# A two-block transformer kernel on one core: a new setup around TensorE, and three waits of the layers put in another order

## The reference, cut to what matters

```python
for l in range(2):
    h = rmsnorm(x, norm_g[l]);  p = split(h @ w_in[l])
    o_a = mla(p.cq, p.ckv, p.krope, ...)            # q = rms(cq) @ w_uq ; k, v = rms(ckv) @ w_ukv
    o_b = diff_attn(p.b_q, p.b_k, p.b_v, ...)
    o_c = dsa(p.c_q, p.c_k, p.c_v, qidx, kidx, widx, topk=128)
    o_d = conv(p.d_b, p.d_c, p.d_h)
    x = x + concat(o_a*silu(gate_a), o_b*silu(gate_b), o_c*silu(gate_c), o_d*silu(gate_d)) @ w_out[l]
x = second_block(x, ...)
```

## Time and profile before

| what | value |
|---|---|
| median of 3 runs | 1811.5 us (1811.14 to 1812.63) |
| the profiled execution's own time | 1812.77 us |
| its span | 1810.9 us |
| PE busy / DVE / ACT / POOL | 99% / 58% / 41% / 22% |
| granted PE clock over the span | 0.997 |
| DMA | 165.53 MB, 91 GB/s over the span |

### The profile page before, as it was taken

How to read it: one execution, slowest core, us unless ns; L and a number is a source line. 1 busy time by engine, 2 the same in 40 slices (tenths; PEclk the granted TensorE clock), 3 DMA queues, 4 the chain that set the end, 5 groups by cost and what they waited for, 6 DMA issues and landing times.

```text
span 1810.9 us, 25324 instructions
## 1 busy us (share of the span) xinstructions
PE 1790.2 (99%) x9372; PEld 1447.0 (80%) x9372; DVE 1051.0 (58%) x2117; ACT 746.6 (41%) x1379; POOL 395.0 (22%) x235
## 2 busy tenths in 40 slices
PE   8999999999999999999999999999999999999998
PEld 5767778776777888888888878878888888888887
DVE  3879767587867764554433435555665655545333
ACT  5454554446455432322222355546444323323222
POOL 2345452444545220000000232130200200000000
PEclk9999999999999999999999999999999999999999
DMA  6222112322211242333333422223221333323332
GB/s 221 71 82 71 59 59 83 95 71 82 76 51 59 86 143 93 98 99 93 97 108 107 154 64 73 91 71 111 87 82 37 103 93 95 102 93 95 103 105 92
DMA packets 49621, 165.53 MB, mean 91 GB/s; under 512 B 5624, under 2 KB 6136, under 8 KB 49528
## 3 DMA queue, kind: packets, MB, share of 16 engines
q1 hardware_dynamic: 48232, 161.88, 28.7%
q10 hardware_dynamic: 1296, 2.42, 0.4%
HBM read 162.12 MB, written 2.17 MB: 91 GB/s over the span
## 4 chain that ended last, share of the span: by engine, by line
PE 93%; DVE 4%; issue 2%; ACT 1%; DMA 0%; POOL 0%; SPq 0%; DVEq 0%; ACTq 0%
PE proj L963 75%; PE o L1237 2%; PE turned L1213 2%; PE score L1187 1%; PE turned L1439 1%; PE score L1430 1%; PE proj L1360 1%; PE o L1465 1%; PE proj L1367 1%; PE score L1196 1%; PE turned L935 1%; PE o L1544 1%; DVE arena L2206 1%; PE turned L947 1%; PE score L1533 1%
## 5 line engine op out<-in xcount | busy, mean ns | idle before, releaser
L963 PE MATMUL proj<-hhi,whi 128*128 128x512 f32 x1464 | 584.9, 400 | 0.6 <-DVE tanh L2123 0.3
L963 PE MATMUL proj<-hhi,wlo 128*128 128x512 f32 x1464 | 571.7, 390 | 0.0
L963 PE MATMUL proj<-hlo,whi 128*128 128x512 f32 x1464 | 570.9, 390 | 0.0
L1632 ACT ACTIVATE whi<-ring 128x1024 fp32r<-128x1024 f32 x280 | 296.2, 1058 | 638.6 <-PE proj L963 632.9
L2068 DVE TENSOR_TENSOR wlo<-ring,whi 128x1024 fp32r<-128x1024 f32 x200 | 244.3, 1221 | 168.2 <-ACT whi L1632 167.6
L963 PEld LDWEIGHTS proj<-hhi,whi 128*128 128x128 f32 x1464 | 275.8, 188 | 59.5 <-issue 6.6
L963 PEld LDWEIGHTS proj<-hhi,wlo 128*128 128x128 f32 x1464 | 275.2, 188 | 58.8
L963 PEld LDWEIGHTS proj<-hlo,whi 128*128 128x128 f32 x1464 | 275.8, 188 | 52.9
L732 POOL TENSOR_TENSOR wlo<-ring,whi 128x1024 fp32r<-128x1024 f32 x80 | 193.5, 2420 | 406.3 <-ACT whi L1632 405.7
L744 POOL TENSOR_TENSOR prob<-prob 128x512 f32<-128x512 f32 x36 | 56.9, 1579 | 877.2 <-ACT prob L1628 877.2
L1658 ACT ACTIVATE prob<-prob,negmax 128x256 f32<-128x256 f32 (+3 forms) x208 | 114.3, 552 | 60.8 <-DVE negmax L2112 59.7
(11 more groups left out here) (304 smaller groups left out, 2394.3 us busy)
## 6 DMA issues: line engine op xcount, KB each, us to landing
ring<-wstream SPq DMA_DIRECT2D x288, 512.0 KB, 3.5
arena<-lines SPq DMA_DIRECT2D x28, 256.0 KB, 5.7
arena<-x ACTq DMA_DIRECT2D x4, 512.0 KB, 6.3
out<-arena SPq DMA_DIRECT2D x8, 256.0 KB, 2.7
arena<-mem SPq DMA_DIRECT2D x1, 1024.0 KB, 9.0
par<-params ACTq DMA_DIRECT2D x3, 74.0 KB, 1.8
arena<-hot SPq DMA_DIRECT2D x2, 80.0 KB
arena<-rope SPq DMA_DIRECT2D x1, 128.0 KB, 7.1
```

The source lines that it names most:

```text
L963: mm = pe.matmul(b, rounded(w), rounded(rhs(v, k)), start=(first and n == 0 and p == 0), stop=(last and n == len(blocks) - 1 and p == 2))
L1632: act.activation(rounded(dst), src, ACT.Copy, scale=scale).then_inc(ready, 1)
```

## The change

Setup: TensorE starts with nine products of the ones tile (`WARM`), into a bank that is written again later, as soon as that tile is set. SP's first weight load no longer waits for x. ACT squares tiles 0 and 1 only, DVE tiles 2 and 3 with its own instruction, and what waited for all four squares waits for two and two. ACT makes the high part of weight slot 0 after the high part of block 0, no longer ahead of it, and TensorE's first job waits for it by a semaphore.

Layers: UQ2 stands ahead of UV0 in `FILLERS`, so both stay in step 5 in the other order, and so do their entries in ACT's and POOL's step 5. `wT` is made right after the keys and has a semaphore of its own (`wt_ready`), on which `turn_w` now waits; `low_idx(1)` comes after the two reads of the rotary keys. DVE runs `low_y` right after the early evictions of its step, ahead of top-k, outputs, gates and late evictions.

```diff
-FILLERS = (... "UK1", "UQ1", "UV0", "UQ2", "UV1", "UQ3", ...
+FILLERS = (... "UK1", "UQ1", "UQ2", "UV0", "UV1", "UQ3", ...
+WARM = 9
...
             for s in range(RING):
-                sp.wait_ge(x_loaded[min(s + 1, NT - 1)], 16)
+                if s:
+                    sp.wait_ge(x_loaded[min(s + 1, NT - 1)], 16)
                 sp.dma_start(ring[:, s, :], wstream[TAKE_FROM[s]]).then_inc(wload[s], 16)
...
-            sp.wait_ge(xsq_ready, NT)
+            sp.wait_ge(xsq_ready, 2)
+            sp.wait_ge(xsq2_ready, 2)
...
+            pe.wait_ge(ones_set, 1)
+            for _ in range(WARM):
+                pe.matmul(turned[0][:, 0:P], ones[:, :], ones[:, :], start=True, stop=True)
...
                 pe.wait_ge(job_free[0], XT_JOB // 2 + 1)
+                pe.wait_ge(hi_ready, 1)
...
                     if k == 4:
-                        wait_out(pe, L, "KR")
+                        pe.wait_ge(wt_ready, L + 1)
...
-                to = (prob, pT)[tok // 2][:, tok % 2 * 2:tok % 2 * 2 + 2, :].rearrange("p a b -> p (a b)")
+                to = prob[:, 2 * tok:2 * tok + 2, :].rearrange("p a b -> p (a b)")
...
-            square_x(2)
-            square_x(3)
-            act.wait_ge(wload[0], 16)
-            make_high(0, 0)
             act.wait_ge(par_loaded, 16)
             for c in range(KC):
+                if c == 1:
+                    act.wait_ge(wload[0], 16)
+                    make_high(0, 0)
                 x_turned(act, c)
...
-            dve.wait_ge(xsq_ready, NT)
+            for tok in range(2, NT):
+                dve.wait_ge(x_loaded[tok], 16)
+                dve.tensor_tensor_reduce(pT[:, 2 * tok - 4:2 * tok - 2, :].rearrange("p a b -> p (a b)"), xnat[:, tok, :], xnat[:, tok, :],
+                                         1.0, 0.0, ALU.mult, ALU.add, ms[:, tok:tok + 1]).then_inc(xsq2_ready, 1)
+            dve.wait_ge(xsq_ready, 2)
+            dve.wait_ge(xsq2_ready, 2)
...
                 scaled(kidxT[32:64, :], src[32:64, :], R[32:64, :]).then_inc(kidx_out, 1)
-                low_idx(1)
-                scaled(wT, src[0:8, :], R[0:8, :], 1.0 / 16)
+                scaled(wT, src[0:8, :], R[0:8, :], 1.0 / 16).then_inc(wt_ready, 1)
                 scaled(krope[HD:HD + 32, 0, :], src[HD:HD + 32, :], R[HD:HD + 32, :])
                 scaled(krope[HD + 32:P, 1, :], src[HD + 32:P, :], R[HD + 32:P, :]).then_inc(job_free[bank_of(L, "KR")], 1)
+                low_idx(1)
                 low_idx(2)
...
                     for name in EARLY[s] if s < FILL_STEPS else ():
                         evict(name)
+                    for n, c in enumerate(Y_ORDER):
+                        if Y_HIGH[c] + 1 == s:
+                            low_y(L * KC + (n + 1), c, yhi)
...
                         if name not in EARLY[s]:
                             evict(name)
-                    for n, c in enumerate(Y_ORDER):
-                        if Y_HIGH[c] + 1 == s:
-                            low_y(L * KC + (n + 1), c, yhi)
```

More of the change, by code:

```diff
@@ L77 @@
         "GT4", "GT5", "DH0", "DH1", "GT6", "GT7") + tuple(f"OUT{c}" for c in range(KC))
-FILLERS = ("BQ1", "VN0", "BK1", "VT1", "UK0", "UQ0", "UK1", "UQ1", "UV0", "UQ2", "UV1", "UQ3", "GT0", "VN1", "GT1", "GT2", "GT3",
+FILLERS = ("BQ1", "VN0", "BK1", "VT1", "UK0", "UQ0", "UK1", "UQ1", "UQ2", "UV0", "UV1", "UQ3", "GT0", "VN1", "GT1", "GT2", "GT3",
            "DB0", "VT2", "DB1", "VN2", "VT3", "SQ0", "SK0", "VN3", "SQ1", "SK1", "SS0", "DC0", "SR0", "DC1", "SR1",
@@ L502, in build @@
         ident_loaded, gain_loaded, par_loaded = sem("ident_loaded"), sem("gain_loaded"), sem("par_loaded")
-        xsq_ready, xt_done, xt_out, xt_out2 = sem("xsq_ready"), sem("xt_done"), sem("xt_out"), sem("xt_out2")
+        xsq_ready, xsq2_ready, xt_done, xt_out, xt_out2 = sem("xsq_ready"), sem("xsq2_ready"), sem("xt_done"), sem("xt_out"), sem("xt_out2")
         tab_loaded = [sem("tab1_loaded"), sem("tab2_loaded")]
@@ L522, in build @@
         kw_ready, kidx_out, kidx_moved = sem("kw_ready"), sem("kidx_out"), sem("kidx_moved")
+        wt_ready = sem("wt_ready")
         relu_ready, idx_added = sem("relu_ready"), sem("idx_added")
```

## The result

The changed kernel takes 1816.1 us in the median of 20 runs (1811.2 to 1821.0), the kernel before 1812.0 in the 20 beside it (1809.8 to 1814.4). The ratio is 1.0022, with a 95% interval of 1.0014 to 1.0030: slower by some 4 us, and above the predicted range. The spread is news too. The kernel before keeps within 5 us, the changed one does not keep within 9, and its median sits between executions that are hardly slower than before and some that lose 9 us.

A forecast was written before the change was run, and what follows sets the result against it. TensorE was taken to bound the kernel, busy 1790.2 of 1810.9 us. Terms -0.1 -1.8 -1.6 +1.6 +3.5 -1.2 +0.1 put +0.5 on 1812.77, 1813.3; carrying half of 1.3 gave 1812.7, range 1808.8 to 1815.0.

The forecast's parts named there:

- UQ2 ahead of UV0, the wait: Second `up_v` of each layer: TensorE idle 2.46 us for ACT's copy of UV0; +1.73 a layer, +3.5 in all.
- `turn_w`: At `turn_w` in each layer: the 0.91 us wait goes, -1.8 in all.
- the old half-clock stretch: Layer 0 behind `turn_w`, from about 43.5 to 47: should go too, -1.6, only in executions that have it.
- `low_y`: Scores of step 28: 0.6 us less waiting a layer, -1.2; steps 34 to 37: +0.1.
- Setup: Before the layers: -0.5 for a clock rising somewhat sooner, +0.4 for weight 0's high part between blocks 0 and 1: -0.1.
- the least case: Setup: the nine products win nothing on the clock; the value taken, -0.5, was near this.
- the first rival: Setup: the clock is up when the transposes begin; setup term -3.3, time 1809.5 us; chance 0.22.
- The sum without new stretches: Whole kernel: all terms on the profiled 1812.77 us, 1813.3, leaving out the +1.6 for a new half-clock stretch.
- the number of new half-clock stretches: Behind the new waits at the second `up_v`: one in two layers, +1.6, bounds 0 and +3.3.
- half of the 1.3 us: Whole kernel: the median, 1811.5, lay 1.3 below the profiled execution; half was carried, taking 1813.3 to 1812.7.
- The third rival: Second `up_v`: the 2.46 us idle is followed by a half-clock stretch in both layers; 1815.4 us; chance 0.12.

The follow-up runs named there:

- the filled wait: The changed kernel with nine overwritten 512-column products put in before the wait of the second `up_v` in each layer: 1812.4 us, ratio 1.0002.
- the parts by themselves: The kernel before with only the `turn_w` and `low_y` parts, `FILLERS` and setup as before: 1807.7 us, ratio 0.9976.
- second profiled execution of the changed kernel: The changed kernel timed again, no line altered: median 1816.9 us, ratio 1.0025; the profiled execution took 1813.51.
- the third's: The changed kernel timed a third time, no line altered: median 1813.9 us, ratio 1.0018; the profiled execution took 1811.75.
- The swap alone: The kernel before with only UQ2 ahead of UV0 in `FILLERS`, timed twice: 1819.1 us, ratio 1.0040, and 1819.2 us, ratio 1.0032.
- the kernel without the ones: The changed kernel with UV0 copied out first by ACT and without the nine products of the ones tile: 1807.1 us, ratio 0.9973.
- the fastest kernel: The kernel before with the `turn_w` and `low_y` parts, UQ2 ahead of UV0, and UV0 copied out first by ACT; old setup: 1806.3 us, ratio 0.9968.
- the kernel with more ones: The changed kernel with UV0 copied out first by ACT, plus six and four more ones products behind the two tables' products: 1809.6 us, ratio 0.9981.

## Why the prediction was wrong

The steps that a single execution shows came out as written, all but one.

- **UQ2 ahead of UV0, the wait: right.** ACT's list puts the two copies and the high part ahead of UV0's copy. The wait is 2.39 us twice, predicted 2.46; as time it costs 3.6 us by the filled wait, predicted 3.5.
- **`turn_w`: right.** Its transposes start at 39.49 with no wait, and the old half-clock stretch behind it is in none of the ten traces of kernels with this edit. What its going is worth stays an estimate, since it was rare before too.
- **`low_y`: right.** In step 28 of layer 0 the scores start at 249.19 with no wait; the waits for row minima fell by 1.7 us in the changed kernel and by 1.4 in the parts by themselves, predicted 1.2. `low_y` got short, and the scaling took over its delay. DVE and POOL in steps 26 and 27 of the changed kernel, against the earlier trace rows:

```profile
240.34 0.68 DVE L2089 TENSOR_TENSOR ylo<-yT,yhi 128x512 fp32r<-128x512 f32 x1
...
244.98 3.04 POOL L833 TENSOR_TENSOR arena<-arena 128x512 f32<-128x512 f32 x2
...
245.68 2.49 DVE L2314 TENSOR_SCALAR prob<-prob,rrow 128x256 f32<-128x256 f32 x2
```

  The scaling's two rose from 1.46 to 2.49 us beside POOL's pair, which fell from 3.44 to 3.04. The Trainium skill (SBUF — State Buffer, Who interferes with whom) has such instructions take turns at a lock; the trace agrees: the scaling's two end at 248.17, just behind POOL's pair at 248.02, and the line's next two, with POOL idle, take 0.75.
- **Setup: the sum within noise, one term missing.** Predicted -0.1; alone it measured some +0.5 (ratio 1.0003), with an interval from -1.1 to +2.2. The clock fell back before the transposes, as the least case had it. The cost between blocks 0 and 1 was smaller than 0.4: from the start of block 0's high part to the start of block 1's low part, 1.99 us became 2.24. What the prediction left out is a wait further on. In the second profiled execution of the changed kernel the clock was up again sooner, and the first job starts 1.85 us ahead of the third's. PE and ACT of the second, then PE of the third:

```profile
16.07 0.47 PE L986 MATMUL proj<-hhi,whi 128*128 128x512 f32 x1 [1.51 <-DVE xT L2135]
...
33.51 1.06 ACT L1640 ACTIVATE whi<-ring 128x1024 fp32r<-128x1024 f32 x1 [5.01 <-DMA ring<-wstream]
...
37.21 0.47 PE L970 MATMUL proj<-hhi,whi 128*128 128x512 f32 x1 [2.14 <-POOL wlo L736]
```

```profile
17.92 0.47 PE L986 MATMUL proj<-hhi,whi 128*128 128x512 f32 x1 [1.51 <-DVE xT L2135]
...
37.08 0.47 PE L970 MATMUL proj<-hhi,whi 128*128 128x512 f32 x1 [0.16 <-POOL wlo L736]
```

  ACT waits for a weight's load, POOL for ACT, and TensorE for POOL, and 20 us later nothing is left of the head start. The swap alone shows the same with the old setup: its first execution starts the first job at 17.20, its second at 18.13, and this product at 36.95 and 36.77. So the first rival, *the warm start holds*, would not have won its 3.3 us either: where the load came soonest with the new setup (ACT starts on it at 32.35 in the kernel without the ones), the product could start near 36.1, 3.7 us behind as in the second execution, and 1.2 sooner than the 37.27 of before (an estimate). In all nine traces with the new setup ACT waits for this load, until 32.4 to 34.7, in three of the five with the old one, until 32.7 to 33.2; whether the new setup delays the load, no run tested.
- **The sum without new stretches: right.** It is 1813.3 - 1.6 = 1811.7; the one profiled execution without any in the layers took 1811.75. Set against the kernel before, the same instructions start 0.1 us sooner behind setup, 2.7 sooner behind the old stretch in layer 0, 0.8 sooner behind `up_v`, 1.5 sooner behind step 28 and 1.3 sooner behind layer 1: each step within some 0.2 us of its term. Another 0.3 came back near 1404, in the second block, which no term has, so the agreement to 0.1 us is in part luck.

**The step that failed is the number of new half-clock stretches**: "I take one new one in two layers, at the old price: +1.6; the bounds are 0 and +3.3." The price was right (1.6 to 1.7 measured, 1.6 said). The count was not, and it was not a constant to be had from one trace. Five executions with this wait show 0, 1, 2, 3 and 4 units, in the layers, and the times of all 41 runs of the changed kernel, 1810.9 to 1821.0, need 0 to five or six at that price. The upper bound of one for each wait failed twice over: a stretch can be a double one, and a further one can come 100 us later, behind narrow products that had kept the clock before. The median of the 20 runs is 4.4 us above the sum without stretches, near three units, where I had one.

A second part of the same step: I took the old stretch out and put one in its place, and then carried half of the 1.3 us by which the median of before lay under its profiled execution, as if the new kernel's stretches were as rare as the old ones. That took off 0.6 where the median needed 2.8 more. From before's own runs, the profiled execution with a stretch looked like the exception it was; nothing in its trace told how often a longer wait would be followed by one: it was seven times in ten.

The third rival, *the new stall costs the clock in both layers*, named the mechanism, the place and the sign, with a chance of 0.12 and a time of 1815.4. It was short by 0.7 us, for the same reason: two stretches were its most.

What stays open: why equal waits, in equal code, bring a low clock in one execution and none in the next. That the stretches behind the two-column products (223 and 537) come of the swap is also not shown: they are in two of the five traces with its unfilled wait, and in none of the nine others, before's included, which speaks for it and settles nothing.

## What to carry to other kernels

A stall of some 2 us in TensorE, where it is otherwise 99% busy, has two prices, its length and what the clock does behind it; here, for two stalls, they were 3.6 and about 3.7 us, so cost both, and treat the second as a spread that takes several executions to see. Before an item moves forward in one engine's order, read what its position sets in the other engines' orders: here a list shared by TensorE and ACT turned a gain of 1 to 1.5 us into a loss of 7, and decoupling the two gave the fastest kernel. A head start in setup is worth only what the next load leaves of it. Filling a stall with idle work tells its two prices apart.

## What the runs showed of the hardware

- One program on one core spreads over 10 us (41 runs, 1810.9 to 1821.0), and its mean granted clock goes from 0.999 to 0.991 along with it. In the three of these runs that were profiled the waits at `up_v` are equal.
- Half-clock stretches in the layers lasted 3.4 us, or twice that, at the low level, and each unit of 3.4 cost 1.6 to 1.7 us in the changed kernel.
- In setup, TensorE worked from 1 to 16 us with one pause of 0.33 us and stayed at the low level throughout, in a mix of ones, 34-row products and transposes; with pauses of 0.16 and 1.37 us, in the changed kernel, it rose for one table's products and fell again. The same eighteen passes of ones were followed by a full clock in six traces and by a low one in two.
- The granted-clock column doesn't always show a low clock in setup: it reads 0.57 for the changed kernel's stretch from 8 to 12, but 1.00 through the setup of the kernel with more ones, as it did before. There only the durations tell.
- The Trainium skill (TensorE: Matmul & The Clock Gate, Part 4: PE-mode transpose) says that the full clock doesn't engage for transposes. The trace differs: in a row of nothing but transposes of x, two take 0.63 us and start 0.43 apart until the clock rises, 0.38 and 0.22 after, and that holds in the changed kernel as in the earlier trace rows.
